# Softmax scaling moved into the product that turns the probabilities, with earlier scores and waits per group

## What is computed

```python
def memory_cross_attention(h, m, wq, wk, wv, q_g, k_g, wo):      # 4 heads of 256
    q = rms_norm((h @ wq).reshape(bsz, L, 4, 256), q_g)
    k = rms_norm((m @ wk).reshape(bsz, 256, 4, 256), k_g)
    ...
    p = jax.nn.softmax(s, axis=-1)
    return jnp.einsum('bhlm,bmhd->blhd', p, v).reshape(bsz, L, 1024) @ wo

# MLA: 8 heads, queries and keys of 96 (64 and 32 rotary), values of 64
# dilated: 4 slots x 3 groups (dilations 1, 4, 16), heads of 64, bias -slope * distance,
#          softmax over the three groups of a slot together; w_out_ab reads both
# GQA: 16 heads of 64 over 4 key heads, then gqa_wo
```

## Time and profile before

| | us |
|---|---|
| median of 3 runs (lowest, highest) | 1224.28 (1222.78, 1228.41) |
| profiled execution, its own time | 1223.7 |
| its span | 1221.7 |
| PE busy in it | 1133.3 (93%) |
| DVE busy | 843.6 (69%) |
| ACT busy | 621.9 (51%) |

### The profile page before, as it was taken

How to read it: one execution, slowest core, us unless ns; L and a number is a source line. 1 busy time by engine, 2 the same in 40 slices (tenths; PEclk the granted TensorE clock), 3 DMA queues, 4 the chain that set the end, 5 groups by cost and what they waited for, 6 DMA issues and landing times.

```text
span 1221.7 us, 20745 instructions
## 1 busy us (share of the span) xinstructions
PE 1133.3 (93%) x7968; PEld 1009.3 (83%) x7968; DVE 843.6 (69%) x1271; ACT 621.9 (51%) x1106; POOL 39.6 (3%) x40
## 2 busy tenths in 40 slices
PE   4899899898999999999988899999988799999998
PEld 4787678698989999999955679999987678999997
DVE  3776674456487877876456477787876657787875
ACT  4633345555454554574454455454564466454554
POOL 2000000010010000010000010000010001000000
PEclk8998899999999999999999999999999899999999
DMA  8343222326257665646430056666586305567650
GB/s 255 113 130 102 72 70 69 104 80 197 68 185 207 176 183 163 199 151 202 132 95 1 12 163 177 167 204 198 180 149 144 87 1 173 145 199 205 174 172 35
DMA packets 218144, 169.18 MB, mean 138 GB/s; under 512 B 20787, under 2 KB 208098, under 8 KB 217954
## 3 DMA queue, kind: packets, MB, share of 16 engines
q1 hardware_dynamic: 216962, 164.44, 46.2%
q0 software_dynamic: 496, 2.43, 0.6%
q10 hardware_dynamic: 624, 1.44, 0.4%
HBM read 167.24 MB, written 1.05 MB: 138 GB/s over the span
## 4 chain that ended last, share of the span: by engine, by line
PE 75%; DVE 13%; ACT 8%; issue 2%; SPq 1%; DMA 1%; POOLq 0%; POOL 0%; DVEq 0%; ACTq 0%
PE bank L2349 19%; PE bank L1988 12%; PE bank L1925 10%; PE bank L2351 10%; PE bank L1926 10%; PE bank L1927 10%; DVE wlo L1312 4%; DVE arena L1305 2%; ACT whi L747 2%; PE bank L1982 1%; PE bank L1983 1%; PE bank L1984 1%; ACT arena L1260 1%; SPq L678 1%; DVE hf L1323 1%
## 5 line engine op out<-in xcount | busy, mean ns | idle before, releaser
L2349 PE MATMUL bank<-mem_pair,whi 128*128 128x512 f32 x1056 | 377.3, 400 | 2.5 <-DVE mem_pair L1622 1.6
L2351 PE MATMUL bank<-mem_pair,wlo 128*128 128x256 f32 x1056 | 296.9, 281 | 0.0
L1925 PE MATMUL bank<-act_hi,whi 128*128 128x256 f32 (+1 forms) x920 | 266.3, 289 | 15.9 <-DVE act_lo L1331 4.7
L1926 PE MATMUL bank<-act_lo,whi 128*128 128x256 f32 (+1 forms) x920 | 262.8, 286 | 0.0
L1927 PE MATMUL bank<-act_hi,wlo 128*128 128x256 f32 (+1 forms) x920 | 262.7, 286 | 0.0
L1312 DVE TENSOR_TENSOR wlo<-raw,whi 128x1024 fp32r<-128x1024 f32 (+3 forms) x137 | 163.3, 1235 | 114.4 <-ACT whi L747 113.3
L2349 PEld LDWEIGHTS bank<-mem_pair,whi 128*128 128x128 f32 x1056 | 199.1, 189 | 49.7 <-DVE mem_pair L1622 2.7
L1697 DVE TENSOR_TENSOR wlo<-raw,whi 128x1024 fp32r<-128x1024 f32 x177 | 208.8, 1220 | 4.0
L2351 PEld LDWEIGHTS bank<-mem_pair,wlo 128*128 128x128 f32 x1056 | 200.0, 189 | 0.1
L1925 PEld LDWEIGHTS bank<-act_hi,whi 128*128 128x128 f32 (+1 forms) x920 | 177.1, 192 | 27.4 <-issue 12.0
L1120 ACT ACTIVATE whi<-raw 128x1024 fp32r<-128x1024 f32 x180 | 179.8, 1046 | 0.4 <-PE bank L1927 0.4
(11 more groups left out here) (215 smaller groups left out, 1309.7 us busy)
## 6 DMA issues: line engine op xcount, KB each, us to landing
raw<-in_ffn_w_in_dram SPq DMA_DIRECT2D x132, 512.0 KB, 5.2
raw<-in_ffn_w_out_dram SPq DMA_DIRECT2D x33, 1024.0 KB, 5.0
raw<-in_w_in_ab_dram SPq DMA_DIRECT2D x11, 1024.0 KB, 6.5
raw<-in_w_in_dram SPq DMA_DIRECT2D x9, 1024.0 KB, 7.4
raw<-in_xa_wk_dram SPq DMA_DIRECT2D x4, 1024.0 KB, 5.5
raw<-in_xa_wv_dram SPq DMA_DIRECT2D x4, 1024.0 KB, 5.0
raw<-in_w_out_dram SPq DMA_DIRECT2D x4, 1024.0 KB, 5.1
raw<-in_xa_wq_dram SPq DMA_DIRECT2D x4, 1024.0 KB, 5.0
```

The source lines that it names most:

```text
L1925: pe.matmul(dst, w[0], a[0], start=start, stop=False, **kw)
L1926: pe.matmul(dst, w[0], a[1], start=False, stop=False, **kw)
L2349: pe.matmul(b[:].rearrange("p (h t) -> p h t", h=2), w[0][:, k, g, :], mem_pair[:, :, k, :], start=k == 0, stop=False, skip_group_check=True)
L2351: last = pe.matmul(b[:, 0:T], w[1][:, k, g, :], mem_hi[:, k, :], start=False, stop=k == KC - 1, skip_group_check=True)
```

## The change

The probabilities are no longer scaled. DVE writes for each head and each half of the queries a diagonal matrix with the reciprocal sums (identity times a column) into `hf`, and PE multiplies with it instead of transposing: the product of a block with the diagonal is the turned and scaled block. The same is done for the dilated units. The remaining edits change the order and the waits: the scores of head 0 stand ahead of the last sum of squares, heads 0 and 1 of MLA ahead of the value tiles; the splits behind `xq` and `mv` stand later; the dilated scores, biases, maxima, exps and values wait per group or half; the output projections wait for their last tiles in the middle of the first product. `DIL_BANKS`, `XA_BANKS` and `turned_bank` only name other banks; MLA has two score banks instead of three.

```diff
+        XA_BANKS = (7, 2, 6, 7)
+        DIL_BANKS = (2, 7, 0)
+        def rescale(a, t):
+            return hf[:, a % 2, t * P:t * P + P]
+        def turned_bank(a):
+            return bank[3 + a % 2 if a < 4 else 4 - a % 2]
         def score_bank(a):
-            return bank[(a + 2) % 3 if a < 12 else a % 4]
+            if a < 4:
+                return bank[XA_BANKS[a]]
+            return bank[a % 2 if a < 12 else a % 4]
...
@@ scalar
             for h in range(4):
-                pair_squares("xq", "xq", 2 * h, h, (("xq", h - 1),) if h else None)
+                pair_squares("xq", "xq", 2 * h, h, (("xq", h - 1),) if h else None, split_last=h < 3)
             rms_from(("xq", 3))
+            after("xq", 7)
...
                 for i in range(count + 3):
+                    if i == 2 and started is not None:
+                        started()
...
-            for i in range(2):
-                evacuate("mv", i, mv[:, i, :], cols=512)
+            def mv_out():
+                for i in range(2):
+                    b = tile_in("mv", i)
+                    act.activation(mv[:, i, :], b[:, 0:512], ACT.Copy).then_inc(ev["act"], 1)
             def dil_exp(s):
-                act.wait_ge(s_dmax, s + 1)
                 for t in range(TT):
+                    act.wait_ge(s_dmax, 2 * s + t + 1)
...
-            attend(4, 8, probs, probsT, MLA_UNITS, lambda: dil_exp(0))
+            attend(4, 8, probs, probsT, MLA_UNITS, mv_out, lambda: dil_exp(0))
+            after("mv", 1)
...
@@ vector
             for h in range(4):
-                for k in range(2):
-                    after("xq", 2 * h + k)
                 mean_square(("xq", h), bank[4][:, 0:T], 256)
                 rms_wait(("xq", h))
                 for k in range(2):
                     scaled(...).then_inc(ev["dve"], 1)
+                after("xq", 2 * h + 1)
...
-                        mul(probs_[:, a % 2, :, :], probs_[:, a % 2, :, :],
-                            rsum[:, a, :].unsqueeze(2).to_broadcast([P, TT, T])).then_inc(s_p, 1)
+                        for t in range(TT):
+                            last = dve.tensor_scalar(rescale(a, t), ident, rsum[:, a, t:t + 1], None, ALU.mult)
+                        last.then_inc(s_p, 1)
...
-            for i in range(2):
-                after("mv", i)
             def dil_bias(s):
-                dve.wait_ge(s_dscore, s + 1)
                 for g in range(3):
+                    dve.wait_ge(s_dscore, 3 * s + g + 1)
...
-                dve.tensor_reduce(nmax[:, 28 + s, :], d, AX.X, ALU.max, negate=True).then_inc(s_dmax, 1)
+                for t in range(TT):
+                    dve.tensor_reduce(nmax[:, 28 + s, t:t + 1], d[:, t, :], AX.X, ALU.max, negate=True).then_inc(s_dmax, 1)
...
-            attend(4, 8, probs, MLA_UNITS, lambda: dil_bias(0))
+            attend(4, 8, MLA_UNITS, lambda: dil_bias(0))
+            after("mv", 1)
...
-                mul(d, d, rsum[:, 28 + s, :].unsqueeze(2).to_broadcast([P, TT, 3 * T])).then_inc(s_dp, 1)
+                for t in range(TT):
+                    last = dve.tensor_scalar(dil_rescale(s, t), ident, rsum[:, 28 + s, t:t + 1], None, ALU.mult)
+                last.then_inc(s_dp, 1)
...
@@ tensor
+                    for tile, value in needs:
+                        if tile == k:
+                            pe.wait_ge(s_olo, value)
...
-            sum_squares(("xq", 3), 0, bank[4][:, 0:T], 2, True, True)
...
-                    if i == count + 1 and ahead is not None:
+                    if i == count and ahead is not None:
                         ahead()
-                        if i >= 3:
-                            pe.wait_ge(s_exp, a - 2)
+                        if i >= reuse:
+                            pe.wait_ge(s_exp, a + 1 - reuse)
...
-                                last = pe.transpose(bank[3 + a % 2][:, m * T + l * P:m * T + l * P + P],
-                                                    probs_[:, a % 2, l, m * P:m * P + P], ident)
+                                last = plain(turned_bank(a)[:, m * T + l * P:m * T + l * P + P],
+                                             probs_[:, a % 2, l, m * P:m * P + P], rescale(a, l))
...
-                evac_wait(pe, "xq", (5, 6, 7, 7)[h])
+                evac_wait(pe, "xq", (1, 5, 5, 7)[h])
...
-            attend(0, 4, cross_scores, cross_values, probs, probsT, lambda i: (i, True))
-            residual_projection("xa_wo", 3, (s_olo, 4))
+            cross_scores(0, score_bank(0)).then_inc(s_score, 1)
+            sum_squares(("xq", 3), 0, bank[4][:, 0:T], 2, True, True)
+            attend(0, 4, cross_scores, cross_values, probs, probsT, lambda i: (i, True), 1, 3)
+            residual_projection("xa_wo", 3, ((0, 3), (6, 4)))
...
-            mla_scores(0, score_bank(4)).then_inc(s_score, 1)
+            for h in range(2):
+                mla_scores(h, score_bank(4 + h)).then_inc(s_score, 1)
...
-                            last = pe.transpose(bank[3 + n % 2][:, m * T + l * P:m * T + l * P + P],
-                                                dprobs2[:, s % 2, l, g * T + m * P:g * T + m * P + P], ident)
+                            last = plain(bank[3 + n % 2][:, m * T + l * P:m * T + l * P + P],
+                                         dprobs2[:, s % 2, l, g * T + m * P:g * T + m * P + P], dil_rescale(s, l))
-                pe.wait_ge(s_dpte, 3 * s + 3)
                 for g in range(3):
+                    pe.wait_ge(s_dpte, 3 * s + g + 1)
...
-            residual_projection("w_out_ab", 5, (s_olo, OHI["dil", 1]))
+            residual_projection("w_out_ab", 5, ((0, OHI["dil", 0]), (5, OHI["dil", 1])))
...
-            residual_projection("gqa_wo", 7, (s_olo, OHI[15]))
+            residual_projection("gqa_wo", 7, ((0, OHI[14]), (7, OHI[15])))
```

More of the change, by code:

```diff
@@ L1065, in pair_squares, with attend @@
                         rms_from(*between)
-                    if plan.ends[name, n0 + k]:
+                    if plan.ends[name, n0 + k] and (k == 0 or split_last):
                         after(name, n0 + k)
             for h in range(4):
-                pair_squares("xq", "xq", 2 * h, h, (("xq", h - 1),) if h else None)
+                pair_squares("xq", "xq", 2 * h, h, (("xq", h - 1),) if h else None, split_last=h < 3)
             rms_from(("xq", 3))
-            def attend(first, count, probs_, probsT_, out_units, ahead=None):
+            after("xq", 7)
+            def attend(first, count, probs_, probsT_, out_units, started=None, ahead=None):
                 for i in range(count + 3):
+                    if i == 2 and started is not None:
+                        started()
                     if i == count + 2 and ahead is not None:
@@ L1660, in _, with attend @@
                            stat_no["xq", h]).then_inc(ev["dve"], 1)
-            def attend(first, count, probs_, out_units, ahead=None):
+                after("xq", 2 * h + 1)
+            def attend(first, count, out_units, ahead=None):
                 for i in range(count + 4):
@@ L1936, in claim, with project @@
                 return ring_bank(name, idx)
-            def project(name, idx, piece, c0, act=None, rows=P, cols=P, h_first=None, x_first=None):
+            def project(name, idx, piece, c0, act=None, rows=P, cols=P, h_first=None, x_first=None, needs=()):
                 b = claim(name, idx, piece)
@@ L2256, in branch_projection, with residual_projection @@
                                 last.then_inc(tile_done, 1)
-            def residual_projection(name, n, h_needed):
-                pe.wait_ge(*h_needed)
+            def residual_projection(name, n, needs):
                 for m in range(KC):
-                    project(name, m, (name, m // 2), P * (m % 2))
+                    project(name, m, (name, m // 2), P * (m % 2), needs=needs if m == 0 else ())
             branch_projection()
@@ L2274, in _, with attend @@
                         sum_squares(("xq", h - 1), 0, bank[4][:, 0:T], 2, True, True)
-            sum_squares(("xq", 3), 0, bank[4][:, 0:T], 2, True, True)
-            def attend(first, count, scores, values, probs_, probsT_, units, started=0, ahead=None, fill=0):
+            def attend(first, count, scores, values, probs_, probsT_, units, started, reuse, ahead=None, fill=0):
                 for i in range(count + 3):
-                    if i == count + 1 and ahead is not None:
+                    if i == count and ahead is not None:
                         ahead()
@@ L2484, in dil_scores @@
                 r = slice(64 * (s % 2), 64 * (s % 2) + 64)
-                if s:
-                    pe.wait_ge(s_dbias, s)
-                else:
-                    pe.wait_ge(s_exp, 12)
                 for g in range(3):
+                    if s:
+                        pe.wait_ge(s_dbias, 3 * s - 2 + g)
+                    elif g == 2:
+                        pe.wait_ge(s_exp, 11)
                     c = 2 * g + s // 2
                     for l in range(TT):
```

(6 more changed lines are left out.)

29 lines of the change are left out of this document (15 added, 14 removed).

## The result

The changed kernel takes 1218.53 us (median of 8 runs, 1212.24 to 1220.72) against 1224.66 us before (8 runs): ratio 0.9931, 95% interval 0.9912 to 0.9951. Predicted were 1219.2 us. A repeat of the same kernel further down has a median of 1213.9 us, so the agreement within 1 us is partly luck. The profiled execution took 1219.0 us, its span 1217.0 us, 4.7 us less than before.

What follows compares the result with a forecast made beforehand. PE bounds the kernel, with 75% of the span, and its gaps are what can be won. Cross attention +3.1, MLA and dilated units -6.9, GQA -0.9 make -4.7 us; forecast 1219.2 us, range 1214 to 1224.

Steps and rivals of the forecast that it cites:

- A turned head: Attention heads: turning by products takes 8 records at 0.1175 us, 0.94 us instead of about 0.46, +0.48 us.
- Rival C: Turning products: each record's 128x128 load sets the pace at 0.19 us; +13.9 us, 1233 us in all; chance 0.04.
- rival D: Turning products: transposes 4x faster in f32, so each product costs 0.43 us; +18.7 us, 1238 in all; chance 0.02.
- A: Faster: PE keeps its clock over the cross attention's gap (-1.65 us), records cost 0.108 us (-1.8); 1215.6 us; chance 0.25.
- E: Early scores don't bring MLA's first maximum forward; some 3 us of the 5.1 are lost; 1222.2 us; chance 0.04.
- Cross attention: Turning 0 +0.9 us, four turned heads +1.9, wait before `xa_wo` -1.35: +1.45 us; with the clock +3.1.
- I take the loss of 3.3 us at half clock, 1.65 us: Cross attention: a 4.0 us gap of PE lowers the clock, costing 1.65 us; ends 0 and 2.4 us.
- MLA: Turning 0 5.1 us earlier without a gap, turning 0 to 2 another -0.6; first dilated turning -4.2 us.
- Dilated units: Units take 8.4 us, PE idles 0.75 us before the last instead of 2.31; with MLA -6.9 us to `w_out_ab`.
- within 0.5%: Whole kernel: change in time below 6.1 us, neither under 1218.2 nor over 1230.4 us; chance 0.55.
- It stays full after the gaps of 2.23 and 2.31 us: PE before the change: granted clock stayed full after these gaps but fell to 0.50 after 3.37 and 3.19 us.
- Rival B: Clock also falls in the 2.2 us gap before unit 0 (+1.6), longer in cross attention (+0.8); 1221.6 us; chance 0.20.

## Why the prediction was right

**A turned head.** Predicted 8 records and +0.48 us; measured 8 and +0.45 (heads 2.96 us apart, before 2.51), 0.11 us a record. Rival C (a load of 190 ns for each) and rival D are out; so are A, since the clock did fall in the cross attention, and E, since MLA's first turning came forward in full. The Trainium skill ("TensorE: Matmul & The Clock Gate", Terms) has the 4x for f32 transposes on which D rested; the trace with transposes put back shows 0.45 us less of 0.90, so 2x.

**Cross attention.** Turning 0 was to come 0.9 us later: 0.57. Without the clock the stage was to take +1.45 us; the kernel with the pause filled has 22.26 - 21.44 = +0.8. The step that was mis-sized is "I take the loss of 3.3 us at half clock, 1.65 us": in the profiled run the lower clock lasted 6.8 us and cost 24.94 - 22.26 = 2.7 us, above my upper end of 2.4; in the second profile 1.5 us. The two errors nearly cancel, and the stage came out at +3.5 for +3.1: that is luck.

**MLA.** Turning 0: -5.1 predicted, 14.78 - 9.51 = -5.3 measured from the third query tile; turning 0 to 2: -0.6, and 4.72 against 5.49 = -0.8. That this hangs on the queue of ACT and DVE, as the prediction had it, the kernel with the split first shows. From turning 2 to the first dilated unit I had +1.6 us, and it was 22.89 against 22.19, +0.7: turning 7 ended 0.25 us sooner, and the chain behind it took 6.0 us instead of 6.6. The pause there was 1.42 us, not 2.2.

**Dilated units.** Unit 0 to `w_out_ab`: 28.8 us predicted, 28.81 measured; 8.45 us a unit for 8.4; last pause 0.50 for 0.75.

**GQA and the others.** -0.77 for -0.9; `xa_wo` and `w_out_ab` without a pause, as the kernel with the waits alone shows too.

**The total.** The span fell by 4.7 us, as the sum says, but not by the same terms: the stages missed by +0.4 and -1.2 us, GQA by +0.1, and +0.7 came from elsewhere. The number given does not quite follow from the sum either: 1219.0 us and the 0.6 us to the median make 1219.6, not 1219.2. The two medians of this kernel, 1218.5 and 1213.9, show how far such a hit can be trusted; the second lies just outside the range of 1214 to 1224. And "within 0.5%", which had the largest chance, is at best a near miss: the ratio of the first set is 0.9931, with 0.9951 as the upper end of the interval.

**What was wrong in the reasoning.** "It stays full after the gaps of 2.23 and 2.31 us", taken as a rule by length, is refuted: the kernel with only the diagonals fell behind that same pause of 2.23 us, the one with only the waits behind 2.31 us (682 to 689 us), the changed one in its second profile behind 1.42 us. Rival B's mechanism exists; it took turns with the cross attention's longer fall. And the gain was not made by what the change is built round: its order and waits alone are worth 15 us (1210.9 against 1226.0 by the median, 1176.3 against 1191.7 by span times clock; 12.6 by the stages with the loss to the clock taken off), and its diagonals give 5 us (by stage, measured alone) to 7 (by stage, within the change; 9 by span times clock) of them back. The prediction had both signs, not the conclusion.

## What to carry to other kernels

Where engines run fixed lists, ask of every late maximum or exp what stands ahead of it in its queue, and on what that waits: moving one weight split was worth 5 us in the cross attention, 2.7 of them from the clock, and with ACT's two copies 4 to 6 us in MLA, and it added no work. Price a fused product by PE's records against the pause it closes: on the engine that sets the end, a cheaper DVE step pays only where PE waits for DVE. And before believing a median that moved by 3 us, add up by stage what the clock took.

## What the runs showed of the hardware

- The granted clock falls in portions: behind 40 us of the span, in every profile, a stretch costs 1.70 or 3.41 us of clock (3.4 or 6.8 us at 0.50), save the last one near the end of the span. The same pause of 3.67 us cost 3.41 in one profile and 1.70 in another of the same kernel.
- In the cross attention and from MLA to `w_out_ab`, over all twelve profiles, the clock fell at each of the ten pauses of PE of 3.17 us or more, at 7 of the 20 between 1.24 and 2.70 us, and at none under 1 us. The same pause of 1.42 us brought it down in two profiles of five, that of 1.77 us in two of three.
- Before 250 us, where no edit reaches, two patterns of falls come up, 5 us apart in time: the last `xq` product starts at 292.4 to 293.5 us or at 287.2 to 288.9. A faster kernel can thus look slow, and did (diagonals only: +0.2 us by the median for +5.3 by stage). What picks the pattern stays open.
- 32 records of products of ones in 3.73 us kept the clock at 1.00 over a pause that otherwise brought it down.
